# In the gated MLP every third load is a modulation tile: the tiles move to one slot of the weight ring, and the first one's products to the stage ahead

## The reference

```python
sh1, sc1, gt1, sh2, sc2, gt2 = ada_params(c[:, None, :], w_ada[layer], b_ada[layer])  # silu(c) @ w + b, split in 6
x = x + gt1 * (jnp.concatenate([y_hy, y_na], axis=-1) @ w_mix_out[i])
x = x + gt2 * swiglu(modulate_2(rmsnorm(x, g_ffn), sh2, sc2), ffn_w1[i], ffn_w3[i], ffn_w2[i])

def swiglu(h, w1, w3, w2):                       # w1, w3: 1024 x 2816, w2: 2816 x 1024
    return (jax.nn.silu(h @ w1) * (h @ w3)) @ w2
```

## Time and profile before

| what | value |
|---|---|
| median of 3 runs | 2568.52 us (2563.57 to 2569.42) |
| profiled execution, its own time | 2569.07 us |
| span of the profiled execution | 2567.8 us |
| mean granted TensorE clock | 0.960 of 2.4 GHz |
| DMA, HBM read | 625.47 MB, 245 GB/s over the span |
| `ffn` stage, PE's first matmul to the residual step behind its last | 1233.76 to 1446.90 us |

### The profile page before, as it was taken

The page is one execution under the profiler, slowest core; times in us unless marked ns, Lnnn a source line. Parts: engine busy times, 40 slices in busy tenths (PEclk is TensorE's granted clock), DMA queues, the critical chain, the costliest instruction groups (busy, mean ns, idle before and its releaser), DMA issues.

```text
span 2567.8 us, 27662 instructions
## 1 busy us (share of the span) xinstructions
PE 2421.1 (94%) x11091; PEld 1796.0 (70%) x11093; DVE 1795.1 (70%) x2019; ACT 1225.9 (48%) x1453; POOL 403.3 (16%) x434
## 2 busy tenths in 40 slices
PE   6977999998899999999997989999999999999998
PEld 2455798544479876454896658787878787877786
DVE  4575577675459765454675338888888888888888
ACT  1142553222145331122433337776767676767775
POOL 1045370131037210153231000000000000000000
PEclk9978999996999999999998999999999999999999
DMA  7631478551156776203465329989898989898995
GB/s 299 269 148 50 170 277 309 208 198 59 47 197 250 302 291 258 90 1 153 175 234 226 126 107 333 367 322 367 322 370 321 369 321 368 322 369 303 364 349 217
DMA packets 50671, 631.01 MB, mean 246 GB/s; under 512 B 8695, under 2 KB 9384, under 8 KB 12712
## 3 DMA queue, kind: packets, MB, share of 16 engines
q1 hardware_dynamic: 44192, 619.47, 63.9%
q10 hardware_dynamic: 3960, 6.97, 0.8%
q0 software_dynamic: 2384, 2.73, 0.3%
HBM read 625.47 MB, written 3.67 MB: 245 GB/s over the span
## 4 chain that ended last, share of the span: by engine, by line
PE 79%; DVE 10%; DMA 3%; ACT 3%; issue 3%; POOL 1%; ACTq 0%; SPq 0%; DVEq 0%; POOLq 0%
PE psum L1136 17%; PE psum L1137 17%; PE psum L1138 17%; PE psum L1031 4%; PE psum L1004 4%; DVE sbuf L701 3%; PE psum L2459 3%; PE psum L2453 2%; PE psum L1220 2%; PE psum L2038 1%; DVE ring_r L1131 1%; DMA ring<-in_t_ada 1%; PE psum L2948 1%; PE psum L1171 1%; PE psum L741 1%
## 5 line engine op out<-in xcount | busy, mean ns | idle before, releaser
L1137 PE MATMUL psum<-ring_r,sc_r 128*128 128x512 f32 x1688 | 666.1, 395 | 0.0
L1131 DVE TENSOR_TENSOR ring_r<-ring,sbuf_r 128x2048 fp32r<-128x2048 f32 (+1 forms) x287 | 539.6, 1884 | 177.6 <-ACT sbuf_r L1122 176.1
L1122 ACT CAST sbuf_r<-ring 128x2048 fp32r<-128x2048 f32 (+1 forms) x287 | 445.5, 1555 | 352.2 <-PE psum L1138 252.5
L1131 DVE TENSOR_TENSOR ring_r<-ring,sc_r 128x2048 fp32r<-128x2048 f32 (+1 forms) x243 | 476.1, 1965 | 148.7 <-ACT sc_r L1122 147.2
L1122 ACT CAST sc_r<-ring 128x2048 fp32r<-128x2048 f32 (+1 forms) x243 | 397.9, 1642 | 277.9 <-PE psum L1138 202.9
L1136 PE MATMUL psum<-sbuf_r,sc_r 128*128 128x512 f32 (+1 forms) x1148 | 429.4, 374 | 18.1 <-DVE sc L2782 17.0
L1137 PEld LDWEIGHTS psum<-ring_r,sc_r 128*128 128x128 f32 x1688 | 317.8, 188 | 73.2 <-issue 3.1
L701 DVE SCALAR_TENSOR_TENSOR sbuf<-ring,sbuf 128x512 f32<-128x512 f32 x404 | 331.4, 828 | 22.6 <-DMA ring<-in_t_ada 17.1
L1138 PE MATMUL psum<-sbuf_r,sc_r 128*128 128x512 f32 x860 | 340.6, 396 | 0.0
L1136 PE MATMUL psum<-sc_r 128*128 128x512 f32 x828 | 333.4, 403 | 0.6 <-DVE sc_r L2980 0.6
L1138 PE MATMUL psum<-sc_r 128*128 128x512 f32 x828 | 324.3, 392 | 0.0
(11 more groups left out here) (333 smaller groups left out, 2896.1 us busy)
## 6 DMA issues: line engine op xcount, KB each, us to landing
ring<-in_t_moe SPq DMA_DIRECT2D x168, 2048.0 KB, 7.9
ring<-in_t_ada SPq DMA_DIRECT2D x48, 2048.0 KB, 9.4
ring<-in_t_mlp SPq DMA_DIRECT2D x32, 2048.0 KB, 8.2
ring<-in_t_win SPq DMA_DIRECT2D x17, 2048.0 KB, 9.8
ring<-in_t_ffn SPq DMA_DIRECT2D x16, 2048.0 KB, 8.7
ring<-in_t_out SPq DMA_DIRECT2D x7, 2048.0 KB, 8.1
ring<-in_t_bias SPq DMA_DIRECT2D x2, 2048.0 KB, 10.0
spectra<-sc POOLq DMA_DIRECT2D x5, 512.0 KB, 3.0
```

The source lines that it names most:

```text
L1122: p.act.e.copy(p.r(hi), src).then_inc(*p.sig("high", st.tag, n))
L1131: p.dve.e.tensor_tensor(p.r(src), src, p.r(hi), ALU.subtract).then_inc(*p.sig("lowp", st.tag, n))
L1137: e.matmul(out, l[0], r[1], start=False, stop=False)
```

## The change

```diff
         loads += [("fu", 0), ("gm", 0), ("bias", 0), ("bias", 1), ("out4", 0), ("out4", 1)]
-        loads += self.among("ffn", range(17), 2, range(42, 48))
+        loads.append(("ada", 42))
+        loads += self.among("ffn", range(17), 3, range(43, 48))
         loads += [("cs", 0), ("out6", 0), ("out6", 1)]
...
     dve_turn(p, "hy", p.HT, 4, [0, 1])
+    dve_products(p, 8, 43)
...
 def pool_mix(p):
-    pool_seed(p, 42)
+    pool_seed(p, 43)
...
-FFN_PRODUCTS = {**{n: 1 for n in range(2, 10)}, **{n: (2, 2, 1, 1, 1, 1, 0, 0)[(n - 12) % 8] for n in range(12, 50)}}
-FFN_SUMS = {13: 43, 21: 44, 29: 45, 37: 46, 46: 47, 52: 48}
+FFN_PRODUCTS = {n for n0 in (2, 17, 29, 41, 53) for n in range(n0, n0 + 8)}
+FFN_SUMS = {2: 43, 13: 44, 27: 45, 40: 46, 50: 47, 61: 48}
...
-        dve_products(p, FFN_PRODUCTS.get(n, 0), 48)
+        if n in FFN_PRODUCTS:
+            dve_products(p, 1, 48)
         dve_columns(p, FFN_SUMS.get(n - 2, 0))
```

## The result

The changed kernel takes 2552.48 us, the median of 5 runs (2551.15 to 2556.27), against 2568.52 for the kernel before: a ratio of 0.9947, 95% interval 0.9933 to 0.9962. The same kernel, run again beside the first three experiments, took 2554.44 us against 2568.44 for the kernel before (ratio 0.9941, 0.9928 to 0.9954). The prediction was 2554.5.

What follows compares the result with a forecast made beforehand. PE, busy 94% of 2567.8 us, was taken to bound the kernel, stalled by late loads. Savings of 3.0 (up pieces) and 11.4 (crossing) less 0.4 (last sum) give 14.0 us: 2568.52 to 2554.5, range 2550.0 to 2560.

Steps and rivals of the forecast that it cites:

- What bounds the kernel: PE, busy 94%; the root of its stalls is SP's queue, waiting 72.7 us for modulation products in the `ffn` stage.
- Part 1: Load order in the `ffn` stage: MLP tiles land before their first casts, least margin 2 pieces, 5.6 to 5.7 us.
- A few: Sign in the trace: SP's waits for products (L701) fall from 72.7 us to a few.
- Part 2: Up pieces of the `ffn` stage: PE's waits for late low parts go, saving 3.0 us, lower bound 2.
- Part 3: Crossing at piece 44: PE's 14.4 us wait for the gating product shrinks to 3.0, saving 11.4 us.
- The clock: After the remaining 3.0 us gap piece 44 still runs slow at 1.2 GHz; its 1.6 us loss stays, no term.
- Part 4: End of the `ffn` stage: PE waits for the last modulation sum after piece 61, cost 0.4 us, bounds 0.2 and 1.5.
- Part 5: Border ahead of the `ffn` stage: eight moved products, 6.25 us on DVE, are hidden, cost 0.
- (b): Rival at piece 44: PE's clock stays up over the shorter gap, giving 2552.9 us; chance 0.12.
- (d): Rival in the `ffn` stage: stalls only move, as products wait for modulation tiles; 2566 to 2570 us, chance 0.04.
- (c): Rival: colliding loads or late DVE in steps 29-36 hold SP past P(39), lengthening the crossing; 2559 us, chance 0.08.
- (e): Rival at the border: residual delayed behind `ada42`'s products, kernel slower by 7.7 us if it lands at 1233; chance 0.03.

Runs made afterwards that it cites:

- the first three experiments: e1, e2 and e3, run in one set with the kernel before (median 2568.44 us) and the repeat of the changed kernel.
- e5: Changed kernel with `ada45`'s products in steps 34 to 41 instead of 29 to 36, `ada46`'s one step later, sums after pieces 45 and 52: 2563.42 us.
- e7: Changed kernel's loads, with `ada42`'s products back in the stage (steps 0 to 6) and the other tiles' from steps 11, 22, 33, 44, 55: 2578.06 us.
- e1: Kernel before, with the last gating product moved ahead of the low part of piece 48 in DVE's step 43: 2558.83 us.
- e4: Changed kernel with modulation tiles after every two MLP tiles, so no fixed slot; `ada42` stays first, other products one per step in steps 2 to 41: 2557.63 us.
- e2: Changed kernel, with the last gating product moved ahead of the low part of piece 48 in DVE's step 43: 2548.02 us.
- e3: e2 plus the last modulation tile's products two per step in steps 53 to 56, its sum after piece 58 instead of 61: 2549.41 us.
- e6: Changed kernel with `ada42`'s eight products done twice at the border, 6.25 us more DVE work: 2553.48 us.

## Why the prediction was right

**What bounds the kernel (right).** The root was SP's wait for a product: e5 puts it back and the gain goes, e7 lengthens the wait and PE's stalls grow with it. The link at the other end is shown by itself: e1 leaves the load late and breaks only the link between low part 48 and the gating product.

**Part 1, the order of loads (right).** No cast after piece 3 waits for a load, and `ffn12` was issued at 1356.12, 12.3 us ahead of P(43) at 1368.4. "A few" was too low for SP: it still waits 23.2 us, four times, for products. They cost nothing, since the loads behind them are not due, which is what the margin of two pieces was to say. e5 took that margin away (five steps against two pieces) and shows where it ends. The 47.9 us of the earlier trace rows were not all of ACT's waits for loads, as I had taken them: two more casts, into `sbuf_r`, waited 10.9 us. None of the eight waits is left.

**Part 2, the up pieces (right).** 3.04 us measured, 3.0 forecast. One reading was loose. I had called the 3.0 us, which PE's weight loads waited for low parts, another wait than the 17.0 for the gating product. They are the same two gaps: the weight loads at 1331.31 and 1356.95 waited 1.09 and 1.86 us, the matmuls behind them at 1331.34 and 1356.98 waited 0.91 and 1.69, and those last ones ended on the gating product, which stands behind a late low part in DVE's stream, as at the crossing. Since I counted the gaps once, the sum was not hurt.

**Part 3, the crossing (right, 0.4 off).** The remaining gap is 3.39 us. 0.3 us of the difference is the low part of piece 48, which took 1.53 us here, and 1.23 at the place from which my 2.99 us were read; 0.1 is the time from PE's end to the cast. What I had not seen is DVE's own lateness: with `ffn12` in place and the tiles ahead of it late 5.7 us of stall stay (e4, and the estimate from e1). The forecast was right in size since the change gets all tiles there in time.

**The clock (right).** After the 3.39 us gap PE's matmuls show 0.63 us, the granted clock is 0.50 from 1371.8 to 1375.0 us (the lower level, 1.2 GHz), and piece 44 takes 4.61 us. e2 gives the price at this place: with a gap of 1.49 us the same piece takes 3.07 at a granted clock of 1.00. The Trainium skill, TensorE: Matmul & The Clock Gate, section Why this matters for your kernels, advises against idle gaps between bursts; this trace agrees for the gap of 3.39 us. In e1 a gap of 1.84 us was enough.

**Part 4, the sums (right).** PE waits 0.35 us (forecast 0.4, bounds 0.2 and 1.5). The 0.15 us for two signals had no row behind it; here PE starts at 1424.81, 0.06 us after DVE's last product ends. And e3 has no such wait, with a stage 0.7 us shorter. The rest of the down part is 0.6 us longer, so 0.25 us of it I can't name.

**Part 5, the border (right, its marks badly set).** The border's length is unchanged to 0.01 us, and the residual's first step stands 17.87 us after the copy of the turned rows, 17.86 before. `ada42` landed 13.0 us after its issue, 13.3 forecast. The casts of pieces 0 to 3 ended at 1218.78 us, 15.62 after that copy; the forecast of 1215 is 14.66 after it, so they were 1.0 us later than forecast. That cost nothing, as DVE was still in the products until 1216.3. But three marks that I gave as times of the trace were missed: a first matmul by 1234.5 (1236.59), which I had made a sign of being wrong, a residual within 1 us of 1218.20 (1221.03), and a stage that ends near 1433 (1436.46). 2.8 us of each is the execution, which was later by that well ahead of the border. They should have been counted from a mark in the same stage.

**The rivals.** (b) is refuted by the slow matmuls, and (d) by the lengths. (c) and (e) did not come up in this kernel. e5 shows the mechanism of (c) once a sum is five pieces late: 10.9 us. e6 bounds (e): 6.25 us of lateness on DVE cost 1.65.

What stays open: the 2.4 us less behind the stage in the profiled execution, why e3, with the shorter stage, is not faster than e2 in time, and why e1 and the kernel before, with the same instructions up to step 43, had gaps of 1.84 and 1.69 us at the same place.

## What to carry to other kernels

When loads stand in one queue and a slot is freed by another engine's work, write down for each load when its slot comes free and when it is due: the gain here was a margin, not the pattern of slots, and five steps of DVE undid 10.9 of its 13.3 us. When an engine waits for a result, look first at what stands ahead of that result in its in-order engine; moving one instruction in the old kernel gave 8.5 of the whole change's 13.3 us, and in the new one another 3.4 us. State what you expect of a trace as lengths between marks in one stage, since positions shift between executions.

## What the runs showed of the hardware

The shortest gap that a slow stretch followed here was 1.84 us, less than the 2.15 of the prediction, and the slow stretch did not always begin when PE resumed. In e1, after a gap of 1.84 us, the 256-column matmuls took 0.28 us up to 1358.96 and then 0.42 up to 1362.32 (granted clock 1.00 in 1357.7 to 1358.9 us and 0.50 in 1359.0 to 1362.3). After the gap of 1.69 us at the same place in the kernel before they stayed at 0.28, with a granted clock of 1.00 up to 1360.0.

```profile
1357.70 0.36 PE L1136 MATMUL psum<-sbuf_r,sc_r 128*128 128x256 f32 x1 [1.84 <-DVE sc L2783]
...
1359.12 0.42 PE L1138 MATMUL psum<-sbuf_r,ring_r 128*128 128x256 f32 x1
```

Later in e1, after the gap of 3.78 us, the first matmuls took 0.40 us, and the level fell only at 1376.14, 1.5 us later:

```profile
1375.65 0.40 PE L1137 MATMUL psum<-ring_r,sc_r 128*128 128x512 f32 x1
...
1376.14 0.63 PE L1136 MATMUL psum<-sbuf_r,sc_r 128*128 128x512 f32 x1
...
1379.54 0.39 PE L1138 MATMUL psum<-sc_r 128*128 128x512 f32 x1
```

Loads in line land later, the more bytes are in front of them. At the border of the changed kernel `ada42`, behind one tile of 2 MB, landed 13.0 us after its issue, and `ffn0`, behind two, 17.4 us, against 8.3 for a lone one. The window of 1203 to 1209 us (its last two numbers are the DMA engines' share and GB/s) shows them full at 431 GB/s. At that rate a tile of 2.1 MB takes 4.9 us, an estimate, and the second and third load in the line took 4.7 and 4.4 us more than the one before:

```profile
1203.00:1209.00 6.00, 5.61 (x15) 2.58 (x14) 0.76 (x2) 0.37 (x2) 0.00 (x0) 1.00 1.02 431
```
